# Query and key projection of the grid heads with exchanged operands, bias loads moved forward, and eight staging buffers for values

## The reference

```python
for l in range(DEPTH):
    h = rms_norm(x, g_mix[l])
    proj = h @ w_in[l]
    p_a, p_b, p_c = ...                      # columns of proj
    pc = p_c.reshape(b, s, 3, HEADS_C, HEAD_DIM)
    o_c = neighbourhood_attention(pc[:, :, 0], pc[:, :, 1], pc[:, :, 2], rpb[l])
    ...
    x = x + mixed @ w_out[l]
    h2 = rms_norm(x, g_mlp[l])
    x = x + jnp.square(jax.nn.relu(h2 @ w_mlp_in[l])) @ w_mlp_out[l]
return rms_norm(x, g_final)

# neighbourhood_attention: for each block of 8 rows x 16 columns of queries
sc = jnp.einsum('bnmiphd,bnmjqhd->bnmhipjq', qg, kg) * (d ** -0.5)
sc = jnp.where(mask, sc + bias, NEG_INF)
o = softmax(sc) @ vg
```

## Time and profile before

| what | value |
|---|---|
| median of three runs | 2915.98 us |
| the profiled execution's own time | 2917.04 us |
| its span | 2915.0 us |
| TensorE matmul busy | 2846.7 us, 98% |
| VectorE busy | 1719.3 us, 59% |
| ScalarE busy | 1056.8 us, 36% |
| mean granted TensorE clock | 0.994 |
| cqk in layer 0 | from about 208 to 255.4 us |
| cv in layer 0 | from 255.4 to 278.9 us |

### The profile page before, as it was taken

The page is one execution under the profiler, slowest core; times in us unless marked ns, Lnnn a source line. Parts: engine busy times, 40 slices in busy tenths (PEclk is TensorE's granted clock), DMA queues, the critical chain, the costliest instruction groups (busy, mean ns, idle before and its releaser), DMA issues.

```text
span 2915.0 us, 39907 instructions
## 1 busy us (share of the span) xinstructions
PE 2846.7 (98%) x14640; PEld 2433.6 (83%) x14640; DVE 1719.3 (59%) x2998; ACT 1056.8 (36%) x1976; POOL 141.3 (5%) x253
## 2 busy tenths in 40 slices
PE   8999999999999999999999989999999999999998
PEld 7998888878888888888798978888788888888886
DVE  6642788885555555455666337788755555555457
ACT  5322777773211111111234237777732111111113
POOL 0001230000000000000000012300000000000000
PEclk9999999999999999999999999999999999999999
DMA  5656874322011111111146577743221111111111
GB/s 196 197 176 173 201 187 111 89 68 99 31 57 43 43 58 43 43 58 50 55 173 208 167 189 179 178 102 87 73 73 44 45 56 43 43 58 43 43 62 70
DMA packets 182359, 285.34 MB, mean 98 GB/s; under 512 B 48848, under 2 KB 138576, under 8 KB 172496
## 3 DMA queue, kind: packets, MB, share of 16 engines
q1 hardware_dynamic: 171600, 254.16, 30.0%
q0 software_dynamic: 10624, 29.41, 3.6%
HBM read 210.60 MB, written 72.88 MB: 97 GB/s over the span
## 4 chain that ended last, share of the span: by engine, by line
PE 85%; DVE 5%; issue 3%; DMA 3%; ACT 2%; DVEq 1%; SPq 0%; ACTq 0%; POOLq 0%
PE ps L1466 24%; PE ps L1281 20%; PE ps L1481 18%; PE ps L1361 7%; PE ps L1375 6%; PE ps L1407 5%; PE ps L1417 2%; PE ps L1247 1%; DMA biasC<-in_bias_c 1%; PE ps L1323 1%; DMA values<-vst 1%; PE ps L1400 1%; DVE x L1200 1%; DVE vbuf L1187 1%; ACT rbuf L871 1%
## 5 line engine op out<-in xcount | busy, mean ns | idle before, releaser
L1481 PE MATMUL ps<-w_dn,hid 128*128 128x512 f32 x3072 | 713.6, 391 | 1.4
L1466 PE MATMUL ps<-hT,w_up 128*128 128x512 f32 x3072 | 702.5, 389 | 3.3 <-DVE hT L921 3.3
L1481 PEld LDWEIGHTS ps<-w_dn,hid 128*128 128x128 f32 x3072 | 573.5, 188 | 132.6 <-DVE x L1200 14.0
L1466 PEld LDWEIGHTS ps<-hT,w_up 128*128 128x128 f32 x3072 | 576.1, 188 | 123.2 <-ACT rbuf L871 3.7
L1281 PE MATMUL ps<-ws,hT 128*128 128x384 f32 (+3 forms) x3072 | 608.3, 356 | 7.5 <-DVE hT L921 5.3
L1281 PEld LDWEIGHTS ps<-ws,hT 128*128 128x128 f32 x3072 | 534.9, 190 | 53.8 <-DVE hT L921 5.8
L1200 DVE TENSOR_TENSOR x<-ps,x 128x512 f32<-128x512 f32 x512 | 343.0, 689 | 223.9 <-PE ps L1481 223.6
L1187 DVE TENSOR_TENSOR vbuf<-rbuf 128x512 f32<-128x512 f32 x128 | 88.5, 692 | 371.0 <-ACT rbuf L871 371.0
L821 ACT ACTIVATE pT<-ps 128x512 fp32r<-128x512 f32 (+1 forms) x448 | 240.6, 582 | 143.1 <-PE ps L1375 141.3
L921 DVE TENSOR_TENSOR pT<-ps,pT 128x512 fp32r<-128x512 f32 (+1 forms) x448 | 281.5, 664 | 7.3 <-ACT pT L821 6.2
L871 ACT ACTIVATE rbuf<-ps 128x512 f32<-128x512 f32 x128 | 76.6, 598 | 553.9 <-PE ps L1466 553.9
(11 more groups left out here) (85 smaller groups left out, 2173.0 us busy)
## 6 DMA issues: line engine op xcount, KB each, us to landing
raw<-in_wstream SPq DMA_DIRECT2D x76, 1024.0 KB, 4.9
head<-feats SPq DMA_DIRECT2D x192, 256.0 KB, 6.4
feats<-tst SPq DMA_DIRECT2D x128, 192.0 KB, 2.6
values<-vst POOLq DMA_DIRECT2D x32, 384.0 KB, 3.1
head<-values SPq DMA_DIRECT2D x24, 512.0 KB, 3.9
biasC<-in_bias_c SPq DMA_DIRECT2D x16, 768.0 KB, 11.4
raw<-in_wstream SPq DMA_DIRECT2D x12, 768.0 KB, 6.0
x_park<-x SPq DMA_DIRECT2D x16, 512.0 KB, 8.3
```

What stands on the lines that cost most here:

```text
L1466: last = pe.matmul(ps[:, k % 2, :], w_up[slot_of(l, 1 if first else 0)][:, w1, kt, ft * P:(ft + 1) * P], hT[:, w2, kt, sh * 512:(sh + 1) * ...
L1481: last = pe.matmul(ps[:, 2 + m % 4, :], hid[slot_of(l + 1, slot)][:, w1, ft, s * P:(s + 1) * P], w_dn[slot_of(l, 0 if last_group else 1)][ ...
```

## The change

The grid heads' cqk tiles are computed with the operands exchanged: the stationary operand is 128 columns of the weights, the moving one 512 tokens of hT. Tile s holds features (s mod 4) x 128 and after for tokens (s div 4) x 512 and after, so that it comes out transposed. For the queries (s mod 4 below 2) the moving operand is read in block order by `by_block`, four blocks of 8 rows by 16 columns. ScalarE copies the bank to `tst` with the scale, VectorE writes the remainder, and two DMAs a tile store it. The "turn" events of cqk are gone.

cv tiles get a buffer each, `cvst`, in the room that latT, vst and part of stage have; the first cv copy waits for all earlier value stores. `first_head` waits only for the stores up to the latent heads' features; it loads the features and values of head 0 at the first cv tile, and the table and both bias halves of head 1 at the second. After cv, SyncE waits for the `feats` stores, loads the features of head 1, and then waits for the value stores.

```diff
     for s in range(ST):
         ev.append(("acc", "cqk", s))
-        if s:
-            ev.append(("turn", "cqk", s - 1))
...
-ACT_FREES = ("a", "uq", "uk", "cqk")
+ACT_FREES = ("a", "uq", "uk")
...
+STORED = [e for e in EVENTS if e[:2] == ("acc", "cqk") or e[0] == "turn" and e[1] != "lat"]
+A_STORED = max(n for n, e in enumerate(STORED) if e[1] in ("uq", "ur", "uk")) + 1
...
+    cvst = sb("cvst", [P, ST, 4, 2 * HD], f32r, "R0", 12 * KB)
...
+        def by_half(ap):
+            return ap.rearrange("p (b f s) -> p b f s", b=4, f=2)
+
         def by_block(ap):
-            return ap.rearrange("p (b r c) -> p b r c", r=2, b=4)
+            return ap.rearrange("p (r b c) -> p b r c", r=8, b=4)
+
+        def value_stage(e, vt):
+            return cvst[:, e[2], :, :] if e[1] == "cv" else vst[:, vt % 2, 0:HA, :]
+
+        def staged(k, w):
+            return tst[:, k, w, :, :].rearrange("p k s -> p (k s)")
...
                     for k in range(NTS):
-                        sp.wait_ge(tst_out[k], (l * TST_N[k] + stores_before(k, turn)) * 16)
+                        sp.wait_ge(tst_out[k], (l * TST_N[k] + stores_before(k, A_STORED)) * 16)
...
                     load_features(l, 0)
+                    load_values(l, 0)
                 elif s == 1:
-                    load_values(l, 0)
+                    sp.dma_start(tabB[:, :], bias_b).then_inc(tab_in, 16)
+                    load_bias(l, 0)
+                    load_bias(l, 1)
...
+                    elif e[:2] == ("acc", "cqk"):
+                        k = turn % NTS
+                        sp.wait_ge(acc_free_dve, l * DVE_FREE_N + frees_before(ACCS.index(e) + 1, False))
+                        hold(sp)
+                        f0, c0 = F_CQ + e[2] % 4 * P, e[2] // 4 * 512
+                        for w in range(2):
+                            rows = feats[w, f0:f0 + P, c0:c0 + 512]
+                            if e[2] % 4 < 2:
+                                rows = by_half(feats[w, f0:f0 + P, :])[:, :, e[2] // 4, :]
+                            sp.dma_start(rows, words(tst[:, k, w, :, :]) if e[2] % 4 < 2 else words(staged(k, w)))\
+                              .then_inc(tst_out[k], 16)
+                        turn += 1
...
                     if n == 1:
-                        stores_done(l)
-                        sp.dma_start(tabB[:, :], bias_b).then_inc(tab_in, 16)
-                    load_head(l, n)
+                        features_done(l)
+                        load_features(l, 1)
+                        values_done(l)
+                    else:
+                        load_head(l, n)
...
+                        elif kind == "cqk":
+                            k = st_turn % NTS
+                            act.wait_ge(acc_done, l * len(ACCS) + acc + 1)
+                            act.wait_ge(tst_out[k], (l * TST_N[k] + TST_BEFORE[st_turn]) * 16)
+                            act.activation(staged(k, HI), bank, ACT.Copy, scale=HD ** -0.5 if s % 4 < 2 else 1.0)\
+                               .then_inc(grid_hi, 1)
+                            st_turn += 1
...
-                            if vt >= 2:
+                            if e == ("acc", "cv", 0):
+                                for k in range(2):
+                                    act.wait_ge(vst_out[k], (l * (len(VSTAGED) // 2) + vt // 2) * 16)
+                            elif vt >= 2 and kind != "cv":
                                 act.wait_ge(vst_out[vt % 2], (l * (len(VSTAGED) // 2) + vt // 2) * 16)
...
+                        elif kind == "cqk":
+                            k = st_turn % NTS
+                            dve.wait_ge(grid_hi, l * ST + s + 1)
+                            if s % 4 < 2:
+                                dve.scalar_tensor_tensor(staged(k, LO), bank, HD ** -0.5, words(staged(k, HI)),
+                                                         ALU.mult, ALU.subtract)
+                            else:
+                                rest(staged(k, LO), bank, staged(k, HI))
+                            dve.drain().then_inc(acc_free_dve, 1)
+                            st_turn += 1
...
+                f, c0 = s % 4 * P, s // 4 * 512
...
-                            mms.append((hT[:, w1, kt, s * P:(s + 1) * P], w_view(l, job, w2)[:, kt, :]))
+                            if kind == "cqk":
+                                tokens = hT[:, w1, kt, c0:c0 + 512]
+                                mms.append((w_view(l, job, w2)[:, kt, f:f + P],
+                                            by_block(tokens) if s % 4 < 2 else tokens))
+                            else:
+                                mms.append((hT[:, w1, kt, s * P:(s + 1) * P], w_view(l, job, w2)[:, kt, :]))
```

More of the change, by code:

```diff
@@ L197, in job_end @@
     return max(n for n, e in enumerate(ACCS) if JOB_OF.get(e[1], e[1]) == job) + 1
-STAGED = [e for e in ACCS if e[1] in ("bq", "bk", "uq", "ur", "uk", "cqk")]
+STAGED = [e for e in ACCS if e[1] in ("bq", "bk", "uq", "ur", "uk")]
 VSTAGED = [e for e in ACCS if e[1] in ("uv", "bv", "cv")]
@@ L206 @@
 TURN = {"bq": ([P] * 3, F_BQ), "bk": ([P] * 3, F_BK), "uq": ([P] * 3, F_AQ), "uk": ([P] * 3, F_AK),
-        "ur": ([P, 96], F_AR), "cqk": ([P] * 4, F_CQ), "lat": ([P] * 3, None)}
-STORED = [e for e in TURNS if e[1] != "lat"]
+        "ur": ([P, 96], F_AR), "lat": ([P] * 3, None)}
+STORED = [e for e in EVENTS if e[:2] == ("acc", "cqk") or e[0] == "turn" and e[1] != "lat"]
+A_STORED = max(n for n, e in enumerate(STORED) if e[1] in ("uq", "ur", "uk")) + 1
 def frees_before(n, act):
@@ L525, in _ @@
                                              words(tst[0:wd, k, :, j, :])).then_inc(tst_out[k], 16)
[L526 to L537, removed]
                         else:
@@ L790, in _ @@
                                 act.activation(tst[0:96, k, HI, 1, :], bank[0:96, P:2 * P], ACT.Copy)
-                                act.drain().then_inc(turn_hi, 1)
-                            elif e[1] == "cqk":
-                                for j in range(2):
-                                    act.activation(by_block(tst[:, k, HI, j, :]), from_grid(bank, j), ACT.Copy)
-                                act.activation(tst[:, k, HI, 2:4, :],
-                                               bank[:, 2 * P:4 * P].rearrange("p (k s) -> p k s", s=P), ACT.Copy)
                                 act.drain().then_inc(turn_hi, 1)
@@ L1032, in _ @@
                             nh = wd // HD
-                            rest(vst[:, vt % 2, 0:nh, HD:2 * HD], bank[:, 0:wd].rearrange("p (h d) -> p h d", d=HD),
-                                 vst[:, vt % 2, 0:nh, 0:HD])
+                            v = value_stage(e, vt)
+                            rest(v[:, :, HD:2 * HD], bank[:, 0:wd].rearrange("p (h d) -> p h d", d=HD), v[:, :, 0:HD])
                             dve.drain().then_inc(acc_free_dve, 1)
@@ L1051, in _ @@
                                 rest(tst[0:96, k, LO, 1, :], bank[0:96, P:2 * P], tst[0:96, k, HI, 1, :])
-                                dve.drain().then_inc(turn_lo, 1)
-                            elif e[1] == "cqk":
-                                for j in range(2):
-                                    dve.tensor_tensor(by_block(tst[:, k, LO, j, :]), from_grid(bank, j),
-                                                      by_block(words(tst[:, k, HI, j, :])), ALU.subtract)
-                                rest(tst[:, k, LO, 2:4, :], bank[:, 2 * P:4 * P].rearrange("p (k s) -> p k s", s=P),
-                                     tst[:, k, HI, 2:4, :])
                                 dve.drain().then_inc(turn_lo, 1)
@@ L1498, in _ @@
                 norm_turn(DEPTH - 1, 3 * ST, t)
-def stores_of(e):
-    return 6 if e[1] == "cqk" else 2
 def stores_before(k, n):
-    return sum(stores_of(e) for e in STORED[k:n:NTS])
-TST_N = [sum(stores_of(e) for e in STORED[k::NTS]) for k in range(NTS)]
+    return 2 * len(STORED[k:n:NTS])
+TST_N = [2 * len(STORED[k::NTS]) for k in range(NTS)]
 TST_BEFORE = [stores_before(n % NTS, n) for n in range(len(STORED))]
```

22 lines of the change are left out of this document (8 added, 14 removed).

## The result

The changed kernel takes 2893.29 us (median of four runs, 2891.39 to 2896.06) against 2916.03 for the kernel before in the same comparison: 22.7 us less, a ratio of 0.9926 with a 95% interval of 0.9914 to 0.9938. The forecast was 2892, and its own range 2887 to 2897. The profiled execution took 2891.39 us with a span of 2889.5.

A forecast was written before the change was run, and what follows sets the result against it. TensorE, busy 98% of the span, bounds the kernel. Gains 7.0 + 7.7 + 10.3 - 1.0 = 24.0 us give 2893.0 profiled, 2892 median; own range 2887 to 2897, 2886 to 2902 for 8 in 10.

The forecast's parts named there:

- Transposes: In cqk, eight groups of four TensorE transposes disappear in each layer, with nothing hiding them: 7.0 us gained.
- Exchanged operands: cqk matmuls with weights stationary and hT moving: 0.8 us possible but not counted; query tiles' runs of 16 taken as zero.
- Rival B: cqk query tiles' moving operand in runs of 16 costs a fixed toll, up to 40 us: 2932; chance 0.06.
- this middle case: Within rival B, 10 ns more for each query-tile matmul in cqk would cost 1.9 us and be lost in the range.
- The start of attention: After cv, eight buffers bring first transposes at 5.56 us, with one hole of some 1.1 us: 7.7 us gained.
- The ninth item: First grid-head attention item: bias and feature waits go, 3.56 us in layer 0, 6.69 in layer 1, together 10.3.
- Rival A: From cqk's end (T) to the ninth item, DMA becomes the bound, 10.8 MB ending at T + 44: 2902; chance 0.20.
- 1.0 kept back: At the ninth item, 1.0 us held back from the gains for features a little late in one layer or the other.
- Rival C: cv holes stay: second item's wait comes from the DMA-starved first head, not its banks; buffers give nothing: 2900; chance 0.05.

The follow-up runs named there:

- the experiment: Changed kernel with another read order of the moving operand in each of the eight cqk tiles, against the changed kernel; one execution, 2896.08 us.

## Why the prediction was right

*Transposes.* As forecast: 7.0 us, nothing hid them.

*Exchanged operands.* This is the mis-sized term. The step took zero for the runs of 16, from the grid scores. Query tiles take 5.74 us against 5.44 contiguous, 12.5 ns a matmul, 8 x 0.30 = 2.4 us. The nearest row could not show it: it is a group of two matmuls, read to 0.01 us. Its pattern, runs of 32 that are 64 apart, cost 5.67 - 5.44 = 0.23 us a tile in the experiment, 9.6 ns a matmul; by an estimate from that, 7 ns for 384 columns, which is 0.014 us for the group. Rival B's mechanism was real, at a sixteenth of its bound of 40 us. The prediction had named this middle case, 10 ns a matmul and 1.9 us, lost in the range; it was 12.5 ns and 2.4 us. Against the 5.48 us of before the query tiles cost 2.1 us and the key tiles give 0.2.

*The start of attention.* 5.56 us forecast, 5.44 and 5.43 measured, with a hole of 1.20 us where 1.1 was named. Gain 7.9, forecast 7.7.

*The ninth item.* All waits gone, 3.56 + 6.69 - 0.43 for the two new holes on VectorE = 9.8 us; booked were 10.3 less 1.0 kept back. Rival A had the load about right: it put 10.8 MB at 257 GB/s into the 42 us up to T + 44, and the trace has 271 GB/s over those 42 us. What it had wrong is that the ninth item needs all of it. It needs the features and the first half of the bias; the features were in at T + 40.0 in layer 0, with 2.9 us to spare (5.2 in layer 1), and the grid values came behind them. The prediction's own argument against A, 16.8 us needed where there are 20, holds: it was 16.5.

Sum of the terms as measured: 7.0 - 1.9 + 7.9 + 9.8 = 22.8 us, against 22.7 for the medians. The two profiled executions differ by 2917.04 - 2891.39 = 25.65; the 2.9 beyond the sum lie outside these steps, 2.7 of them between the end of layer 0's attention and layer 1's cqk, and within the 4.7 us that the four runs of the changed kernel spread. In the two stretches that the change touches the traces differ by 22.7 us. The forecast's 24.0 was made against profiled executions; that the medians lie so near the sum as measured is in part luck, given these spreads.

*What the sum got right by adding, it got right for the whole alone.* It said what each hole cost; it did not say what each edit was worth. The 7.7 us booked to the buffers are 24 us if the buffers are taken away. The 6.8 us of bias waits booked to the early bias are nothing in the trace if it alone is taken away, because the loads that no longer wait for the value stores are in time either way; put behind those stores as well, they cost 10. Rival C was wrong with its premise, since the second item's wait follows the buffers in every version.

## What to carry to other kernels

At a seam where several loads and stores share the DMA engines, the slack belongs to all edits together. Moving loads earlier gained 3.4 us on the old kernel; with two buffers and exchanged operands, where the earlier loads include head 1's features, the same move lost 8 (from -7.1 to +1.2), and with eight buffers it gained 12. So add the buffers before the early loads. Late loads with two buffers, but not behind the value stores, were not tried. Take edits away from the finished version one at a time, and read in the trace whether the seam has changed; adding them to the old one told of 3 and 7 us here where the whole was 23. If a matmul's operand must be permuted, let the evacuation do it when ScalarE and VectorE are idle.

## What was not expected of the hardware

The read order of the moving operand costs time in a way that neither the number of runs nor their distance explains alone: 512 columns in 128 runs of 4 that are 16 elements apart are free (5.42 us a tile), 64 apart they cost 6.67, and runs of 16 cost 5.75 at 32 and 5.74 at 64. Runs of 8 that are 32 apart took 5.53 us in two tiles of a layer and 5.28 to 5.32 in two others. The Trainium skill ("Advanced Engine Details and Errata", Memory Cachelines) has lines of 16 bytes in SBUF and wants at least two hits in each; by that all eight patterns would be free, and this measurement decides otherwise for six of them. And a wait costs more than its length: behind the 6.98 us TensorE's granted clock was 0.50 (1.2 GHz). 14.4 us passed in place of 5.4; 6.65 of the 9.0 us more are waits, and most of the rest is work at the lower clock (4.97 us from the second item's scores to the transposes, against 3.02 without its hole).
